# Reordering the opening of a two-block float32 layer kernel: constants and x first in the load queue, the angles and sines behind the v group, modulation products out of the q and k columns

## The reference, cut to what matters

```
mod = silu(c) @ w_ada + b_ada
shift1, scale1, gate1, shift2, scale2, gate2 = split(mod, 6)
h = rms_norm(x, g_pre_mix) * (1.0 + scale1) + shift1
proj = h @ w_in                       # 1024 x 3584
xin, b_gate, c_gate, q, k, v, g = split(proj, ...)
q = rotary(q, positions);  k = rotary(k, positions) * dh ** -0.5
...
x = x + gate1 * rms_norm(mix @ w_out, g_post_mix)
h = rms_norm(x, g_pre_mlp) * (1.0 + scale2) + shift2
...
```

## Time and profile before

| | us |
|---|---|
| median of 3 runs | 1538.56 |
| the profiled execution's own time | 1538.69 |
| its span, first to last instruction | 1536.9 |
| PE busy | 1467.9 (96%) |
| DVE busy | 874.4 (57%) |
| ACT busy | 557.2 (36%) |
| bytes moved by DMA | 159.06 MB |

### The profile page before, as it was taken

How to read it: one execution, slowest core, us unless ns; L and a number is a source line. 1 busy time by engine, 2 the same in 40 slices (tenths; PEclk the granted TensorE clock), 3 DMA queues, 4 the chain that set the end, 5 groups by cost and what they waited for, 6 DMA issues and landing times.

```text
span 1536.9 us, 18402 instructions
## 1 busy us (share of the span) xinstructions
PE 1467.9 (96%) x7168; PEld 1212.9 (79%) x7168; DVE 874.4 (57%) x1719; ACT 557.2 (36%) x979; POOL 0.2 (0%) x4
## 2 busy tenths in 40 slices
PE   1899999899999999999999899999999999999897
PEld 1677777888888888798888788888888888888676
DVE  3787555553433334665467434524778777787435
ACT  4612123632223223442232323533344444445331
POOL 0000000000000000000000000000000000000000
PEclk9899999999999999999999999999999999999999
DMA  5766322153222223223322222322222222211121
GB/s 194 273 232 237 133 82 97 55 194 140 94 97 98 100 100 110 69 76 106 107 96 83 96 96 83 110 96 82 69 69 70 69 69 69 70 64 64 65 69 55
DMA packets 43717, 159.06 MB, mean 103 GB/s; under 512 B 4848, under 2 KB 5232, under 8 KB 43504
## 3 DMA queue, kind: packets, MB, share of 16 engines
q1 hardware_dynamic: 43632, 157.90, 30.1%
HBM read 155.78 MB, written 2.10 MB: 103 GB/s over the span
## 4 chain that ended last, share of the span: by engine, by line
PE 86%; DVE 6%; ACT 4%; issue 2%; DMA 1%; SPq 0%; ACTq 0%; DVEq 0%
PE PS L445 26%; PE PS L447 26%; PE PS L446 26%; PE PS L729 1%; PE PS L777 1%; PE PS L740 1%; DMA CST<-in_cst 1%; ACT WH L1594 1%; PE PS L781 1%; PE PS L771 1%; DVE WL L923 1%; PE PS L749 1%; PE PS L757 1%; DVE Z L879 1%; PE PS L626 1%
## 5 line engine op out<-in xcount | busy, mean ns | idle before, releaser
L445 PE MATMUL PS<-HH,WH 128*128 128x512 f32 (+1 forms) x1152 | 459.5, 399 | 4.4 <-ACT TMP L1696 2.3
L447 PE MATMUL PS<-HH,WL 128*128 128x512 f32 (+1 forms) x1152 | 437.9, 380 | 0.0
L446 PE MATMUL PS<-HL,WH 128*128 128x512 f32 (+1 forms) x1152 | 436.5, 379 | 0.0
L923 DVE TENSOR_TENSOR WL<-RAW,WH 128x1024 fp32r<-128x1024 f32 x226 | 275.0, 1219 | 92.5 <-ACT WH L1594 92.2
L1594 ACT ACTIVATE WH<-RAW 128x1024 fp32r<-128x1024 f32 x226 | 238.1, 1056 | 195.2 <-PE PS L447 145.0
L445 PEld LDWEIGHTS PS<-HH,WH 128*128 128x128 f32 x1152 | 218.5, 190 | 46.5 <-issue 6.3
L447 PEld LDWEIGHTS PS<-HH,WL 128*128 128x128 f32 x1152 | 218.2, 189 | 42.0
L446 PEld LDWEIGHTS PS<-HL,WH 128*128 128x128 f32 x1152 | 218.8, 190 | 40.3 <-issue 3.6
L445 PE MATMUL PS<-WH,ZH 128*128 128x512 f32 x400 | 156.4, 391 | 3.9 <-issue 3.9
L447 PE MATMUL PS<-WH,ZL 128*128 128x512 f32 x400 | 156.3, 391 | 0.0
L446 PE MATMUL PS<-WL,ZH 128*128 128x512 f32 x400 | 156.2, 391 | 0.0
(11 more groups left out here) (227 smaller groups left out, 1654.7 us busy)
## 6 DMA issues: line engine op xcount, KB each, us to landing
RAW<-in_w_fc SPq DMA_DIRECT2D x64, 512.0 KB, 3.2
RAW<-in_hgrn_in SPq DMA_DIRECT2D x64, 512.0 KB, 3.2
RAW<-in_ada SPq DMA_DIRECT2D x48, 512.0 KB, 4.7
RAW<-in_pool_in SPq DMA_DIRECT2D x40, 512.0 KB, 3.3
RAW<-in_w_in SPq DMA_DIRECT2D x28, 512.0 KB, 4.6
RAW<-in_pool_out SPq DMA_DIRECT2D x16, 512.0 KB, 3.2
RAW<-in_hgrn_out SPq DMA_DIRECT2D x16, 512.0 KB, 3.2
RAW<-in_w_out SPq DMA_DIRECT2D x8, 512.0 KB, 3.3
```

What stands on the lines that cost most here:

```text
L445: e.matmul(out, wh, xh, start=first, stop=False)
L446: e.matmul(out, wh, xl, start=False, stop=False)
L447: return e.matmul(out, wl, xh, start=False, stop=last)
L923: e.tensor_tensor(lo, RAW[:, i % NR, :], hi.bitcast(F32), ALU.subtract).then_inc(taken.sem, taken(i))
```

## The change

- The unit list: in the first part w_in 1, 2 and 3 follow features 0, 2 and 4 (they come with f = 1, 3, 5 instead of 2, 4, 6); w_in 4 to 11 (q and k) have no modulation units between them; w_in 12 to 27 have one behind even and two behind odd numbers, 24 in all.
- SyncE: the constants come second, ahead of the row c and x; the positions move behind unit 19; the mask and the decay matrices come after unit 24; the gate's rows after w_in 10.
- VectorE: squares of token tiles 1 and 3 with their sums, factors, tiles 2 and 3 scaled, the loop (the low halves of w_in 1 to 3 at the end of f = 1, 3, 5), the low half of w_in 4, and only then the angles, the absolute value, w_in 5 and the rotation factors.
- ScalarE: squares of tiles 0 and 2, the high half of w_in 0 ahead of the factors, tiles 0 and 1 scaled; the sine and the cosine after the high halves of w_in 4 and 5, ahead of the evictions of v.
- TensorE: the same work; it waits for scaled tile 1 of ScalarE instead of 2.

```diff
--- before.py
+++ after.py
@@ -32,14 +32,14 @@
 
     out = []
     for f in range(8):
-        if f % 2 == 0:
-            out.append(("w_in", f // 2, True))
+        if f in (0, 1, 3, 5):
+            out.append(("w_in", (f + 1) // 2, True))
         out += [("ada", 2 * f, False), ("ada", 2 * f + 1, False)]
     ada = iter(range(16, 48))
     for n in range(4, 28):
         out.append(("w_in", n, True))
-        if n <= 24:
-            out += [("ada", next(ada), False) for _ in range(2 if 12 <= n < 15 else 1)]
+        if n >= 12:
+            out += [("ada", next(ada), False) for _ in range(1 + n % 2)]
     for name, n in (("w_out", 8), ("w_fc1", 32), ("w_fc2", 32), ("pool_in", 40), ("pool_out", 16),
                     ("hgrn_in", 64), ("hgrn_out", 16)):
         for i in range(n):
@@ -354,21 +354,21 @@
                 e.dma_start(to, a["rows"][i].partition_broadcast(128)).then_inc(s_row, 16)
 
             e.dma_start(VEC[:, :], a["vec"]).then_inc(s_vec, 16)
+            e.dma_start(CST[:, :], a["cst"][:, 0:C_D]).then_inc(s_cst, 16)
             e.dma_start(flat(0), a["rows"][5].partition_broadcast(128)).then_inc(s_c, 16)
-            e.dma_start(POSI, a["positions"].partition_broadcast(128)).then_inc(s_pos, 16)
             for t in range(4):
                 e.dma_start(X[:, t, :], a["x"][128 * t:128 * t + 128, :]).then_inc(s_x[t], 16)
-            for i in range(NR):
+            for i in range(20):
                 load(i)
-            e.dma_start(CST[:, :], a["cst"][:, 0:C_D]).then_inc(s_cst, 16)
-            for i in range(NR, 22 + NR):
+            e.dma_start(POSI, a["positions"].partition_broadcast(128)).then_inc(s_pos, 16)
+            for i in range(20, 20 + NR):
                 load(i)
             e.dma_start(MSK[:, :], a["msk"]).then_inc(s_msk, 16)
             e.dma_start(DMASK, a["cst"][:, C_D:C_N].rearrange("p (h t) -> p h t", h=4)).then_inc(s_d, 16)
-            for i in range(22 + NR, len(UNITS)):
+            for i in range(20 + NR, len(UNITS)):
                 load(i)
 
-                if UNITS[i][0:2] == ("w_in", 8):
+                if UNITS[i][0:2] == ("w_in", 10):
                     e.wait_ge(hlo.sem, hlo.of("in", 7))
                     row(flat(0), 0)
                     row(flat(2), 1)
@@ -602,7 +602,7 @@
 
             e.wait_ge(own.sem, own.of("ones"))
             e.wait_ge(s_cst, 16)
-            e.wait_ge(normed.sem, normed.of("x", 2))
+            e.wait_ge(normed.sem, normed.of("x", 1))
             e.wait_ge(own.sem, own.of("normed", "x", 3))
             for f in range(4):
                 first_tokens(f)
@@ -1019,7 +1019,7 @@
 
             def token_factors(stage, t0, n):
 
-                e.wait_ge(square.sem, square.of(stage, "x", t0 + n - 1))
+                e.wait_ge(square.sem, square.of(stage, "x", 2 if stage == "x" else t0 + n - 1))
                 e.tensor_scalar(NW[:, 4, 0:n], SSX[:, t0:t0 + n], EPS, None, ALU.add).then_inc(own.sem, own())
                 e.wait_ge(own.sem, own.n)
                 root(RT[:, t0:t0 + n], n)
@@ -1108,6 +1108,33 @@
             e.wait_ge(s_c, 16)
             e.wait_ge(copied.sem, copied.of("silu row"))
             e.tensor_tensor(CB[:, :], flat(2), flat(0), ALU.mult).then_inc(own.sem, own("cb"))
+            for t in (1, 3):
+                e.wait_ge(s_x[t], 16)
+                e.scalar_tensor_tensor(out=flat(2 + 2 * t), in0=X[:, t, :], scalar=1.0 / 1024, in1=X[:, t, :],
+                                       op0=ALU.mult, op1=ALU.mult, accum_out=SSX[:, t:t + 1]).then_inc(
+                                           own.sem, own("squares", t))
+            e.wait_ge(own.sem, own.of("squares", 3))
+            token_factors("x", 0, 4)
+            normed_tokens("x", 2)
+            normed_tokens("x", 3)
+
+            def first_low(k):
+                e.wait_ge(hhi.sem, hhi.of("in", k))
+                e.tensor_tensor(HL[:, k, :], TMP[:, 2 + k % 2, :], HH[:, k, :].bitcast(F32),
+                                ALU.subtract).then_inc(hlo.sem, hlo("in", k))
+
+            p.next, p.hi, p.unit = 20, 4, 4
+            lo_to(1)
+            for f in range(8):
+                first_modulation(f)
+                if f:
+                    first_low(f - 1)
+                if f in (1, 3, 5):
+                    lo_to((f + 3) // 2)
+            first_low(7)
+            lo_to(5)
+
+
             e.wait_ge(s_pos, 16)
             e.wait_ge(s_cst, 16)
             e.tensor_copy(TN, POSI).then_inc(own.sem, own())
@@ -1122,31 +1149,14 @@
                 e.wait_ge(own.sem, own.n)
                 e.scalar_tensor_tensor(out=ANG, in0=TN, scalar=-part, in1=ANG, op0=ALU.mult,
                                        op1=ALU.add).then_inc(own.sem, own())
-            token_factors("x", 0, 4)
-            normed_tokens("x", 3)
-
-            def first_low(k):
-                e.wait_ge(hhi.sem, hhi.of("in", k))
-                e.tensor_tensor(HL[:, k, :], TMP[:, 2 + k % 2, :], HH[:, k, :].bitcast(F32),
-                                ALU.subtract).then_inc(hlo.sem, hlo("in", k))
-
-            p.next, p.hi, p.unit = 20, 4, 4
-            for f in range(8):
-                if f % 2 == 0:
-                    lo_to(f // 2 + 1)
-                first_modulation(f)
-                if f:
-                    first_low(f - 1)
-                if f == 1:
-                    e.scalar_tensor_tensor(out=TN, in0=ANG, scalar=-1.0, in1=ANG, op0=ALU.mult,
-                                           op1=ALU.max).then_inc(own.sem, own("angle"))
-            first_low(7)
-            lo_to(5)
+            e.wait_ge(own.sem, own.n)
+            e.scalar_tensor_tensor(out=TN, in0=ANG, scalar=-1.0, in1=ANG, op0=ALU.mult,
+                                   op1=ALU.max).then_inc(own.sem, own("angle"))
+            lo_to(6)
             e.wait_ge(copied.sem, copied.of("cos"))
             e.tensor_tensor(TN, SIN, SIN, ALU.mult).then_inc(own.sem, own())
             e.scalar_tensor_tensor(out=SIN, in0=SIN, scalar=CST[:, C_SGN:C_SGN + 1], in1=COS,
                                    op0=ALU.mult, op1=ALU.mult).then_inc(own.sem, own())
-            lo_to(6)
             e.wait_ge(own.sem, own.n)
             e.tensor_scalar(COS, TN, -2.0, 1.0, ALU.mult, ALU.add).then_inc(own.sem, own("rot"))
 
@@ -1766,17 +1776,18 @@
             e.activation(COL[:, 8:16], VEC[:, V_C:V_C + 8], ACT.Sigmoid).then_inc(copied.sem, copied("silu"))
             e.wait_ge(s_c, 16)
             e.activation(flat(2), flat(0), ACT.Sigmoid).then_inc(copied.sem, copied("silu row"))
-            for t in range(4):
+            for t in (0, 2):
                 e.wait_ge(s_x[t], 16)
                 token_squares("x", t)
+            hi_to(1)
             e.wait_ge(own.sem, own.of("factors", "x", 0))
-            for t in range(3):
-                normed_tokens("x", t)
+            normed_tokens("x", 0)
+            normed_tokens("x", 1)
             e.wait_ge(own.sem, own.of("gb"))
             for f in range(8):
                 b = 4 + f % 4
-                if f % 2 == 0:
-                    hi_to(f // 2 + 1)
+                if f in (1, 3, 5):
+                    hi_to((f + 3) // 2)
                 e.wait_ge(taken.sem, taken.of(UNITS.index(("ada", 2 * f, False))))
                 e.activation(GA[:, f:f + 1], MOD[:, 8 + f:9 + f], ACT.Identity,
                              scale=VEC[:, V_GPRE1 + f:V_GPRE1 + f + 1], bias=GB[:, f:f + 1]).then_inc(
@@ -1792,13 +1803,12 @@
                              bias=MOD[:, f:f + 1]).then_inc(banks.free[b], 1)
                 e.wait_ge(*banks.taken(("x", "t", f)))
                 e.activation(HH[:, f, :], TMP[:, 2 + f % 2, :], ACT.Copy).then_inc(hhi.sem, hhi("in", f))
-                if f == 2:
-                    e.wait_ge(own.sem, own.of("angle"))
-                    e.activation(SIN, ANG, ACT.Sin, scale=0.5)
-                    e.activation(COS, TN, ACT.Sin, scale=-0.5, bias=CST[:, C_HPI:C_HPI + 1]).then_inc(
-                        copied.sem, copied("cos"))
             hi_to(6)
             p.unit = 4
+            e.wait_ge(own.sem, own.of("angle"))
+            e.activation(SIN, ANG, ACT.Sin, scale=0.5)
+            e.activation(COS, TN, ACT.Sin, scale=-0.5, bias=CST[:, C_HPI:C_HPI + 1]).then_inc(
+                copied.sem, copied("cos"))
 
 
             def values(j):
```

## The result

The changed kernel takes 1526.84 us (median of 4 runs, 1525.97 to 1529.81) against 1538.18 us before (4 runs, too); the ratio is 0.9929, 95% interval 0.9909 to 0.9949. That is 10.9 us by the ratio, where 17.5 was forecast (1521.2): faster, but by less than two thirds of it. The median lies just inside the forecast range (1516.5 to 1527.0); by the ratio the time is 1527.3 us, just outside it.

A forecast was written before the change was run, and what follows sets the result against it. TensorE was taken to set the pace from 72 us on, the constants' wait and then VectorE before it. v group 17.0 + columns 1.0 - sines 0.5 = 17.5 us; 1538.7 - 17.5 = 1521.2 us, range 1516.5 to 1527.0.

The forecast's parts named there:

- part 1: Opening: early constants, angles moved away and squares on two engines start the first low half at 17.1, 13.3 us earlier.
- part 2: Loop of eight features: 34.2 us instead of 37.9, with 6.4 us of waits, ending at 51.3; 3.7 us gained.
- I follow a burst as 3.2, then 1.26 for each more: Loads in the loop: a burst's first piece lands after 3.2 us, each further piece 1.26 us later.
- the sign that the prediction had set for itself (over 38 us): Loop of eight features: the prediction would be wrong if the loop takes over 38 us.
- Rival (b): Loop: loads set the pace, each burst sharing the 16 engines and taking 5.2 us; gain 11.5 us, 1527.2 us; chance 0.18.
- w_in n is two products further back on VectorE: Loop: given as a remedy for waits on high halves made directly ahead of VectorE's use, within 9.5 us of waiting before.
- part 3: Behind the v group: angles and sines run later, nearly hidden, with 0.3 us to spare; 0.5 us lost.
- part 4: Columns: no modulation in q and k, 24 products in the 16 columns after; 1.0 us gained, within -0.5 to 1.4.
- rival (e): g, x, c and b columns: slow loads in the ring of five delay VectorE, then TensorE; slower, 1546.8 us; chance 0.02.
- rival c: Last two features of the v group: gaps bring TensorE's clock to 1.2 GHz, 5.4 us more, 1526.6 us; chance 0.1.

The follow-up runs named there:

- Experiment 3: The kernel before with only its load of the constants moved to second place in the queue: 1530.01 us, ratio 0.9939.
- experiment 7: The changed kernel with all four squares and three scaled tiles back on ScalarE: 1525.63 us, ratio 0.9924.
- Experiments 1, 2 and 6: The changed kernel with w_in 1 to 3 taken in list order, 1518.87 us; nine buffers for 20 pieces, 1516.97 us; list alone put in taking order, 1517.35 us.
- Experiment 5: The changed kernel with w_in 1 to 3 back at features 2, 4 and 6 in the list and both engines' turns: 1524.53 us, ratio 0.9915.
- Experiments 8 to 10: The changed kernel with later modulation pieces spread and the gate row's matmuls later: with nine buffers 1512.62 us, list in taking order 1514.6 us, alone 1523.01 us.
- experiment 4: The changed kernel with one modulation piece per q and k column again and the gate's rows behind w_in 8: 1529.02 us, ratio 0.9934.
- experiment 10: The changed kernel with only the later modulation pieces spread and the gate row's matmuls in the next column: 1523.01 us, ratio 0.9897.

## Why the prediction was right or wrong

**The front (part 1) was right.** The factors started at 13.59 (14.0), the loop at 16.71 (17.1), 13.7 us earlier where 13.3 was forecast. Experiment 3 shows what carries it: the constants' place in the queue, 10.7 us. The squares on two engines, which I let matter in the text, are not among the causes (experiment 7); the rest is that ScalarE makes the high half of w_in 0 before the factors, so that VectorE doesn't wait 3.4 us for it. That ScalarE scales one tile less isn't needed for this: in experiment 7 it scales three, and the loop starts at 15.56.

**The loop (part 2) is where the prediction failed.** The mechanism was in it: the load waits in SyncE's queue for w_in n, and loads leave in bursts. The term that failed is "I follow a burst as 3.2, then 1.26 for each more". In the trace the first piece of a burst took 3.7, 3.8 and 4.2 us. In the first two bursts the second landed 1.2 to 1.3 us behind it, as forecast, but the third 2.2 and 2.6 us behind the second; in the last burst the second was already 2.4 us behind the first. For the earlier of its two late pieces VectorE waited 2.1, 2.2 and 1.4 us (forecast 1.9, 1.9, 0.6), and then again for the later one 1.0, 1.4 and 1.2 us, where I had 0 to 0.2. That makes 9.2 us of waits instead of 4.6, nearly all of the 4.8 us that the loop was too long by. At 39.0 us the loop also passed the sign that the prediction had set for itself (over 38 us). The 1.26 us came from the opening, where the queue was full throughout. In a burst the pieces in flight seem to share the engines: an estimate from the rates between 25.0 and 31.5 us is 2.1 MB, four pieces of the five, moved when the third was reported.

Rival (b) had this, with 0.18; it should have had more, since its own row, 5.2 us in a full stream, was a row of the same loop. That its time came out so exactly (1527.2 for 1527.3) is partly luck: it had 5.2 us for the first piece of a burst, the loop was too long by 4.8 us and not by 6, and the columns below made up the difference.

The late pieces close a circle: w_in n is taken after the products on the two pieces that its own lateness delays. The prediction followed it with its own numbers, 9.0 us to a turn. In the trace a turn is the third landing of a burst and VectorE's start on it (7.3 us), a product, a feature low and a weight low (1.15 + 0.6 + 1.15), about 10.2 us, and the low halves of w_in 1, 2 and 3 came 10.3 and 10.6 us apart (at 23.06, 33.33, 43.95), for 6.9 us of VectorE's work. What I did not see is that the change itself had made the circle: "w_in n is two products further back on VectorE" is true only against the list. VectorE's order stayed as it was, and the list was moved away from it. Experiments 1, 2 and 6 open the circle in three ways and the loop is 29 to 31 us each time. Experiment 5 against experiment 3 gives the sines' move: 1.7 us (37.9 to 36.2), of which 0.6 is the absolute value that left the loop.

**The sines (part 3): hidden, with more room than forecast.** ScalarE's timeline:

```profile
57.17 1.28 ACT L1809 ACT_TABLE_LOAD   x1
62.62 0.63 ACT L1809 ACTIVATE Z<-Z 128x512 f32<-128x512 f32 x1 [4.16 <-DVE TMP L1153]
63.16 0.71 ACT L1810 ACTIVATE Z<-TMP,CST 128x512 f32<-128x512 f32 x1
63.77 2.04 ACT L1816 ACTIVATE Z<-PS 128x512 f32<-128x512 f32 x4
65.68 2.96 ACT L1604 ACTIVATE WH<-RAW 128x1024 fp32r<-128x1024 f32 x3
```

The table load ran ahead of the wait for the angles, so only 1.15 of the 2.45 us stood behind it. The low half of w_in 6 ended at 68.0, 2.2 us before TensorE's need at 70.2, and TensorE waited for nothing there: 0 instead of the 0.5 that I took.

**The columns (part 4): 1.0 us forecast as gained, 0.8 lost.** TensorE's waits from 57 to 130 and from 130 to 250 us:

```profile
PE PS L409 <- DVE Z L863: 1.6, 1, 1.6
```

```profile
PE PS L590 <- DVE DG L1095: 1.9, 2, 1.1
```

The gate row waits 1.6 us as before (1.4), although it is in a g column. The timelines of ScalarE, VectorE and TensorE tell why:

```profile
120.19 1.06 ACT L1604 ACTIVATE WH<-RAW 128x1024 fp32r<-128x1024 f32 x1 [5.36 <-DMA RAW<-in_w_in]
121.16 0.58 ACT L1824 ACTIVATE Z<-PS 128x512 f32<-128x512 f32 x1
...
121.77 0.69 DVE L1179 TENSOR_TENSOR Z<-Z,PS 128x512 f32<-128x512 f32 x1 [2.44 <-ACT Z L1824]
122.37 1.28 DVE L863 SCALAR_TENSOR_TENSOR Z<-RAW,COL,Z 128x1024 f32<-128x1024 f32 x1
...
123.70 1.98 PE L409 MATMUL PS<-Z,ONES 128*128 128x512 f32 x4 [1.64 <-DVE Z L863]
```

ScalarE waited for a late w_in piece, the sigmoid stood behind it, VectorE's multiply behind the sigmoid, the product behind that. I priced the multiply and not the wait in front of it. The retention norm waits 0.8 us more (1.1 before), because the last two products fall just ahead of its diagonal. Experiments 8 to 10 take both away. That is rival (e) in small. A wait of 0.2 us for a weight's low half is gone, so that of the 1.6 us given back behind the v group 0.8 are these waits. The other 0.8 stay unexplained, and lie within what single executions differ by: with the same two waits and the same instructions behind the v group, experiment 5 took 1463.9 us for the rest and the changed kernel 1466.5. Against the right base part 4 did gain: with parts 1 to 3 in place and part 4 undone (experiment 4) TensorE waited 4.9 us in these columns, with it 3.5. I had priced it against the kernel before, whose gate row waited 1.4 us.

**The clock (rival c) cost nothing at the end of this trace, but did in others.** After TensorE's longest gap, 3.2 us, the granted clock was 0.50 (1.2 GHz) at 46.0 to 47.9 us and full again before the last two features; the group ended 3.7 us after the last low half, as before. Gaps of up to 2.9 us left it at full in this trace. But in experiment 10 it fell to 0.50 after a gap of 2.0 us, in experiment 7 after 2.7, so that no length of gap divides the two. In experiments 4 and 10 it stood at 0.50 in the last two features, and the group ended 5.3 us after the last low half. Rival (c) was right that this can happen, and too high in its price: 1.6 us, where it had 5.4.

In sum, forecast and measured, rounded: start 13.3 and 13.7, loop 3.7 and -1.1, part 3 -0.5 and 0, part 4 1.0 and -0.8, unexplained -0.8; 17.5 and 11.1 us of span.

## What to carry to other kernels

In a ring of buffers fed from an ordered queue, the list must stand in the order in which the buffers are taken, or the ring must be deeper than the difference: a load that waits for a late taker holds up every load behind it, free buffers or not. Before pricing a queue by a rate, look where its loads leave in bursts, and price the second and third landing by a row of a burst, not by a stream. And undo each part of a change alone, and each part's halves: here one moved load gave most of the gain, and in one part the earlier high halves gained 5.9 us of the loop and the early places in the list lost more than that.

## What the runs showed of the hardware

Pieces of 512 KB issued close together don't all land at the step of the opening's stream, 1.26 us: issued from 24.3 to 26.6 us, the five took 3.7, 4.6, 6.4, 7.2 and 7.4 us, the third landing 2.2 us behind the second, while the DMA engines moved 272 to 410 GB/s. The same three bursts in four executions cost VectorE 9.2, 9.0, 7.6 and 6.9 us of waits. And the load of ScalarE's function table isn't held by the wait of the function behind it: it ran at 57.17, 5.4 us before the sine, right behind the instruction ahead of it.
